# Leaving out the products that nothing reads, in the norms of a two-block transformer kernel

## The chip, the cores and the metric

One Trainium2 chip, one core of it. The metric is the device time of one execution of the whole program, in microseconds (us). PE is TensorE, DVE is VectorE, ACT is ScalarE, POOL is GpSimd, SP issues the loads.

## The reference

Two models run one after the other on 272 and then 256 positions of width 1024. The first has two layers: differential attention with a SwiGLU, then a two-way RWKV-7 time mix with a mixture of eight experts; each half of a layer ends in a layer norm. The second has two layers of sparse attention beside a gated linear recurrence, each behind an rms norm, and a last rms norm at the end. The norms that matter here:

```python
def layer_norm(x, g, b):
    mu = jnp.mean(xf, -1, keepdims=True)
    var = jnp.mean(jnp.square(xf - mu), -1, keepdims=True)
    return ((xf - mu) * lax.rsqrt(var + LN_EPS) * g + b).astype(x.dtype)
...
h = layer_norm(DEEPNORM_ALPHA * h + mix, ln_g[i, 0], ln_b[i, 0])
...
h = layer_norm(DEEPNORM_ALPHA * h + ff, ln_g[i, 1], ln_b[i, 1])
...
    ym = jnp.mean(y, -1, keepdims=True)
    yv = jnp.mean(jnp.square(y - ym), -1, keepdims=True)
    y = ((y - ym) * lax.rsqrt(yv + RW_LNX_EPS)).reshape(B, L, D) * lnx_g + lnx_b
...
def rmsnorm(x, g):
    y = xf * lax.rsqrt(jnp.mean(xf * xf, axis=-1, keepdims=True) + NORM_EPS)
```

## The kernel before

The state is kept transposed in SBUF: `H` is 128 partitions x 8 slices x 272 positions, feature on the partition. Every weight comes from HBM in 1 MB loads, ACT rounds a piece to its high part (`wh`, line 301), DVE subtracts to get the low part (`wl`, line 310), and PE makes three products per tile (`mm3`, lines 158 to 160). Four such pieces are kept at a time: ACT may round piece n only when PE has used piece n-4.

A sum over features is a product with a matrix of ones. In a layer norm (`norm_pe`) PE sums `H` (line 436), DVE centres it (L473), ACT squares it (L452), PE sums the squares (L443), DVE scales and adds the epsilon (L479), ACT takes the root (L456), DVE the reciprocal (L481), and DVE and ACT make the eight slices of the next input (L489, L462, L486, L464), on which the next stage's first products wait. The rms norm (`rms_pe`, L2272) is the same without the centring. The norm over heads in the time mix sums squares at L1180, makes the root and reciprocal (L1544, L1321, L1547), and then goes slice by slice: PE spreads the reciprocal (L945), DVE multiplies (L1554, L1557, L1560), PE makes the next gate product (L1187, L1188).

Each of these norms ends, on PE, in a call of `busy_pe`: five (over heads: three) fp32 products of the identity with 512 columns of constants into a PSUM bank. Their semaphore `busy` is waited for only by a later product that takes the same bank.

PSUM has eight banks. `bank()` hands them out in turn, from 0 to 7 and again, unless the caller names one, and returns who held the bank before; the caller waits until that holder's result has been read:

```python
    def bank(event, *key, b=None):
        if b is None:
            b = turn[0] % 8
            turn[0] += 1
        before, holder[b] = holder.get(b), (event, *key)
```

In the attention of the second model the banks are named: scores in 0 and 1, the turned scores in 2, their products with the values in 3, and beside them eight units of `ma` and then `rnn` in 4 to 7 (units 4 to 7 of `rnn` last). `ga`, the eight units ahead of the attention, and `out_a`, the eight behind it, take banks in turn. On DVE the last steps of the attention stand in this order:

```python
            low(dve, SB)
...
            if n in (13, 19):
                for i in range(4):
                    rnn_gate(i + 4 * (n // 19))
```

so `rnn_gate(4)` to `rnn_gate(7)` (L2821), which read the banks of `rnn` 4 to 7, come behind the last two `low` steps (L310). Nothing else orders PE against them before `out_a`: PE waits there for the attention's own result, its weights and its bank. All orders are written out by hand; there is no scheduler.

Of the kernel before, what the change touches and what calls it, by code (L numbers as in the profile page):

```python
# [162 lines left out]
def build(nc, A, out, known=None, stages=99):  # L163
# [15 lines left out]
    def tile(name, cols, dt=F32):  # L179
        o = top[0]  # L180
        top[0] += -(-cols // 8) * 32
        return at_offset(name, o, cols, dt)
# [7 lines left out]
    PAR, CB = tile("PAR", NPAR), tile("CB", 592)  # L190
# [7 lines left out]
    PS = nc.alloc_psum_tensor("PS", [128, 8, 512], F32)  # L198

    ident = CB[:, 0:128]  # L200
# [12 lines left out]
# [5 lines that stand above are left out]
        bank_of[(event, *key)] = b  # L218
        return b, before
# [197 lines left out]
    top[0] = ARENA  # L417
    LNQ, LNR, LNS = tile3("ln_sq", KC, T), tile("ln_r", T), tile("ln_s", T)

    def busy_pe(pe, n, *key, at=None):  # L420

        b, before = bank("busy", *key, b=at)
        if before:
            pe.wait_ge(pe.at(*before))
        for i in range(n):
            t = pe.e.matmul(PS[:, b, :], ident, CB[:, 0:512], start=True, stop=True)
        t.then_inc(*pe.sig("busy", *key))

    def norm_pe(pe, key, after, Tn=T):

        b, before = bank("ln_sum", key)
        if before:
            pe.wait_ge(pe.at(*before))
        for k in range(KC):
            pe.wait_ge(pe.at(after, k))
            t = pe.e.matmul(PS[:, b, 0:Tn], ones, H[:, k, 0:Tn], start=k == 0, stop=k == KC - 1)
        t.then_inc(*pe.sig("ln_mm", key, "sum"))
        b, before = bank("ln_var", key)
        if before:
            pe.wait_ge(pe.at(*before))  # L440
        for k in range(KC):
            pe.wait_ge(pe.at("ln_sq", key, k // 2))
            t = pe.e.matmul(PS[:, b, 0:Tn], ones, LNQ[:, k, 0:Tn], start=k == 0, stop=k == KC - 1)  # L443
        t.then_inc(*pe.sig("ln_mm", key, "var"))
        busy_pe(pe, 5, key)

    def norm_act(act, key, hi=None, st=None):

# [80 lines left out]
    def attention_pe(pe):  # L529
# [74 lines left out]
        for i in range(4, KC):  # L604
            project_unit(pe, SA, "attn_o", i, 128, at_xs, T)
        norm_pe(pe, 0, "attn_o")

    def attention_act(act):
# [159 lines left out]
    def ffn_pe(pe):  # L768
        for _ in project_units(pe, SA, "gate", [("gate", 0), ("gate", 1), ("up", 0), ("up", 1)], ff_x, T, ("x_lo", "ln", 0)):
            pass  # L770
        for f0 in range(2, FFN // 128, 2):
            for what in ("gate", "up"):
                for j in range(2):
                    project_unit(pe, SA, what, f0 + j, 128, ff_x, T)
        for _ in contract_pe(pe, SA, "down", FFN // 128, ff_h, T, ("ff_lo",)):
            pass
        norm_pe(pe, 1, "down")
# [160 lines left out]
    def rwkv_pe(pe):  # L938
# [42 lines left out]
        for u in range(KC + 2):  # L981
            if u == 2:
                b, before = bank("k_norm")
# [11 lines left out]
        for j, w in enumerate([128, 32]):  # L995
            b, before = bank("gate_h", j)
            pe.wait_ge(pe.at(*before))
            for k in range(KC):
                pe.wait_ge(pe.at("mixed", 5, k))
                t = e.matmul(PS[0:w, b, 0:T], gv[:, k, j * 128:j * 128 + w], MIXED[5][:, k, :], start=k == 0, stop=k == KC - 1)  # L1000
# [3 lines left out]
        for f in range(KC):  # L1004
            b, before = bank("k_spread", f)
# [5 lines left out]
        def take(event, *key, b=None):  # L1011
            b, before = bank(event, *key, b=b)
            pe.wait_ge(pe.at(*before))
            return b
# [151 lines left out]
        for c in range(4):  # L1166
            for f in (2 * c, 2 * c + 1):
                take("bonus_v", c, b=f)
                t = e.matmul(PS[:, f, 0:T], blk, bonus[:, f, 0:T], start=True, stop=True)
            t.then_inc(*pe.sig("bonus_mm", c))  # L1170
        pe.wait_ge(pe.at("y", len(groups) - 1))
        for c in range(4):
            for f in (2 * c, 2 * c + 1):
                take("y_mean", c, b=f)
                t = e.matmul(PS[:, f, 0:T], blk, rw_y[:, f, 0:T], start=True, stop=True)
            t.then_inc(*pe.sig("y_mean_mm", c))
        b = take("y_var", b=0)
        for f in range(KC):
            pe.wait_ge(pe.at("y_sq", f // 2))
            t = e.matmul(PS[0:16, b, 0:T], by_head[:, f, :], po_q[:, f, :], start=f == 0, stop=f == KC - 1)  # L1180
# [4 lines left out]
        def gate(f):  # L1185
            b = take("y_gate", f, b=2 + f % 2)
            e.matmul(PS[:, b, 0:T], slot[:, f * 128:(f + 1) * 128], gh[:, 0, :], start=True, stop=False)  # L1187
            e.matmul(PS[:, b, 0:T], slot[0:32, D + f * 128:D + (f + 1) * 128], gh[0:32, 1, :], start=False, stop=True).then_inc(  # L1188
                *pe.sig("y_norm_mm", f, "gate"))

        pe.wait_ge(pe.at("raw", "A", m))
        gate(0)
        gate(1)
        busy_pe(pe, 3, "y", at=1)
        pe.wait_ge(pe.at("y_var_r"))
        first_units = project_units(pe, SA, "rw_o", [("rw_o", i) for i in range(4)], po_y, T, ("x_lo", "rw_o"),
                                    (4, 5, 6, 7))
# [9 lines left out]
        for i in range(4, KC):  # L1207
            project_unit(pe, SA, "rw_o", i, 128, po_y, T)
        norm_pe(pe, 2, "rw_o")

    def rwkv_act(act):
# [1055 lines left out]
    def rms_pe(pe, l):  # L2267
        b, before = bank("rms_sum", l)
        pe.wait_ge(pe.at(*before))
        for k in range(KC):  # L2270
            pe.wait_ge(pe.at("rms_sq", l, k // 2))
            t = pe.e.matmul(PS[:, b, 0:SEQ], ones, rq[:, k, :], start=k == 0, stop=k == KC - 1)  # L2272
        t.then_inc(*pe.sig("rms_mm", l))
        if l < 2:
            busy_pe(pe, 5, "rms", l)

    def rms_act(act, l):
        for c in range(4):
# [32 lines left out]
    def second_pe(pe, l):  # L2311
        e = pe.e
        rms_pe(pe, l)
        for _ in project_units(pe, SB, "iq", [("iq", (l, u)) for u in range(4)], (hh, hl), SEQ, ("x_lo", f"hn{l}")):
            pass
# [141 lines left out]
        if l:  # L2457
            rms_pe(pe, 2)
# [482 lines left out]
    def stage_list(name):  # L2941
        none = lambda x: 0
        lists = {"pe": [attention_pe, ffn_pe, rwkv_pe, moe_pe, none, second_pe],
                 "act": [attention_act, ffn_act, rwkv_act, moe_act, none, second_act],
                 "dve": [attention_dve, ffn_dve, rwkv_dve, moe_dve, none, second_dve],
                 "pool": [none, none, rwkv_pool, moe_pool, none, second_pool]}[name]
        f = lists.pop()
        return (lists + [lambda x: f(x, 0), lambda x: f(x, 1)])[:stages]
# [136 lines left out]
```

## Time and profile before

| | us |
|---|---|
| median of 3 runs | 2882.27 (2877.8 to 2885.52) |
| the profiled execution, its own time | 2887.5 |
| its span, first to last instruction | 2885.7 |
| PE busy | 2687.2 (93%) |
| DVE busy | 2045.1 (71%) |
| ACT busy | 1541.5 (53%) |
| mean granted TensorE clock | 0.957 of full |

A busy share tells how much of the span an engine had work; which engine sets the time of a stretch is read from the waits. The granted clock is full (2.4 GHz) or half (1.2 GHz); a value between is a mean over a stretch.

### The profile page before, as it was taken

To read this page: it belongs to the slowest core of one execution; us is meant where nothing else is said; L and a number is where in the kernel's file an instruction comes from. 1 tells how busy PE (TensorE), PEld (TensorE's weight loads), DVE (VectorE), ACT (ScalarE), POOL (GpSimd) and SP (SyncE) were. 2 spreads that over 40 slices of the span, in tenths; PEclk is the share of its full clock that TensorE was granted. 3 is DMA by queue.
4 is the path that set the end of the run, shared out by engine and by line. 5 is a ranking of instruction groups with operands and counts; after the bars stand their busy time and mean duration, and the time that the engine had idled before them with its cause. 6 is when DMAs were issued, how large, how long until landed. Compare 5 with 4: busy or idle time off the path is not lost.

```text
span 2885.7 us, 49498 instructions
## 1 busy us (share of the span) xinstructions
PE 2687.2 (93%) x21078; PEld 2216.2 (77%) x21078; DVE 2045.1 (71%) x2943; ACT 1541.5 (53%) x2245; POOL 101.4 (4%) x124
## 2 busy tenths in 40 slices
PE   7779999999898999999999999998999989999988
PEld 7649997688876766666666666667969988978977
DVE  4565546664435889898898989895856865757864
ACT  3334442622123777777777777774446454446443
POOL 0000000010003100000000000000000101000001
PEclk9759999999988999999999999999999999999999
DMA  6203553300022799898999989893525634524532
GB/s 206 74 0 117 176 171 98 108 21 4 4 102 75 297 348 349 332 364 335 344 352 348 351 330 364 333 346 102 153 58 149 186 113 123 154 80 145 167 118 96
DMA packets 244413, 547.66 MB, mean 190 GB/s; under 512 B 24492, under 2 KB 187784, under 8 KB 200924
## 3 DMA queue, kind: packets, MB, share of 16 engines
q1 hardware_dynamic: 242204, 541.54, 53.3%
q8 instruction: 169, 2.77, 0.4%
q0 software_dynamic: 1984, 2.89, 0.4%
q14 instruction: 56, 0.46, 0.0%
HBM read 540.46 MB, written 1.05 MB: 188 GB/s over the span
## 4 chain that ended last, share of the span: by engine, by line
PE 75%; DVE 15%; ACT 6%; issue 2%; DMA 2%; DVEq 0%; SPq 0%; ACTq 0%
PE PS L158 20%; PE PS L160 20%; PE PS L159 20%; DVE wl L310 3%; ACT wh L301 3%; PE PS L1066 1%; PE PS L349 1%; PE PS L2379 1%; PE PS L1810 1%; PE PS L577 1%; DVE mix L1359 1%; DMA raw<-in_w_in 1%; DVE mix L1357 1%; PE PS L1836 1%; PE PS L1094 1%
## 5 line engine op out<-in xcount | busy, mean ns | idle before, releaser
L310 DVE TENSOR_TENSOR wl<-raw,wh 128x1024 fp32r<-128x1024 f32 (+2 forms) x630 | 746.3, 1189 | 411.5 <-ACT wh L301 392.7
L301 ACT ACTIVATE wh<-raw 128x1024 fp32r<-128x1024 f32 (+2 forms) x630 | 643.9, 1026 | 582.6 <-PE PS L160 534.5
L310 DVE TENSOR_TENSOR wl<-early,wh 128x1024 fp32r<-128x1024 f32 x384 | 466.8, 1225 | 55.6 <-ACT wh L301 35.2
L301 ACT ACTIVATE wh<-early 128x1024 fp32r<-128x1024 f32 x384 | 407.0, 1061 | 127.7 <-PE PS L160 118.7
L158 PE MATMUL PS<-b_hn_h,wh 128*128 128x256 f32 (+2 forms) x1312 | 378.5, 288 | 15.1 <-DVE wl L310 8.9
L160 PE MATMUL PS<-b_hn_h,wl 128*128 128x256 f32 (+2 forms) x1312 | 372.3, 284 | 0.0
L159 PE MATMUL PS<-b_hn_l,wh 128*128 128x256 f32 (+2 forms) x1312 | 371.7, 283 | 0.0
L158 PE MATMUL PS<-wh,xe_h 128*96 128x512 f32 x896 | 357.3, 399 | 1.2 <-DVE xe_l L1962 1.2
L160 PE MATMUL PS<-wh,xe_l 128*96 128x512 f32 x896 | 353.7, 395 | 0.0
L159 PE MATMUL PS<-wl,xe_h 128*96 128x512 f32 x896 | 353.4, 394 | 0.0
L158 PEld LDWEIGHTS PS<-b_hn_h,wh 128*128 128x128 f32 (+2 forms) x1312 | 233.4, 178 | 20.6 <-DVE wl L310 10.5
L159 PEld LDWEIGHTS PS<-b_hn_l,wh 128*128 128x128 f32 (+2 forms) x1312 | 233.2, 178 | 0.7
L160 PEld LDWEIGHTS PS<-b_hn_h,wl 128*128 128x128 f32 (+2 forms) x1312 | 233.1, 178 | 0.3
L160 PEld LDWEIGHTS PS<-wh,xe_l 128*96 128x96 f32 x896 | 144.8, 162 | 63.6
L158 PEld LDWEIGHTS PS<-wh,xe_h 128*96 128x96 f32 x896 | 145.1, 162 | 61.1 <-DVE xe_l L1962 1.5
L159 PEld LDWEIGHTS PS<-wl,xe_h 128*96 128x96 f32 x896 | 145.4, 162 | 59.3
L158 PE MATMUL PS<-wh,mh_h 128*96 128x512 f32 x448 | 177.8, 397 | 0.0
L160 PE MATMUL PS<-wh,mh_l 128*96 128x512 f32 x448 | 177.0, 395 | 0.0
L159 PE MATMUL PS<-wl,mh_h 128*96 128x512 f32 x448 | 175.8, 392 | 0.0
L158 PE MATMUL PS<-ff_x_h,wh 128*128 128x272 f32 x352 | 102.1, 290 | 0.5 <-DVE ff_x_l L486 0.3
L160 PE MATMUL PS<-ff_x_h,wl 128*128 128x272 f32 x352 | 101.8, 289 | 0.0
L349 PE MATMUL PS<-mix,raw 128*128 128x272 f32 x384 | 95.4, 410 | 6.8 <-DVE mix L1359 4.0
(473 smaller groups left out, 5127.8 us busy)
## 6 DMA issues: line engine op xcount, KB each, us to landing
early<-in_moe_in SPq DMA_DIRECT2D x128, 1024.0 KB, 4.8
raw<-in_moe_in SPq DMA_DIRECT2D x96, 1024.0 KB, 4.8
early<-in_moe_out SPq DMA_DIRECT2D x64, 1024.0 KB, 4.8
raw<-in_w_in SPq DMA_DIRECT2D x56, 1024.0 KB
raw<-in_moe_out SPq DMA_DIRECT2D x48, 1024.0 KB, 4.9
raw<-in_w_in SPq DMA_DIRECT2D x32, 704.0 KB
raw<-in_attn_w_in SPq DMA_DIRECT2D x12, 1024.0 KB, 5.5
raw<-in_rw_w_rkv SPq DMA_DIRECT2D x12, 1024.0 KB, 5.0
```

Of the source, the lines that this page charges most:

```text
L158: e.matmul(o, wh, xh, start=start, stop=False)
L159: e.matmul(o, wh, xl, start=False, stop=False)
L160: return e.matmul(o, wl, xh, start=False, stop=stop)
L301: act.e.activation(st.two(n)[0], st.raw(n), ACT.Copy).then_inc(*act.sig("hi", st.name, n, sem=f"hi_{st.name}"))
L310: dve.e.tensor_tensor(lo, st.raw(n), hi.bitcast(F32), SUB).then_inc(*dve.sig("lo", st.name, n, sem=f"lo_{st.name}"))
L349: t = pe.e.matmul(PS[:, b, 0:Tn], cols_view(256)(st.slot(m))[:, k, c:c + 128], X[:, k, :], start=k == 0, stop=k == KC - 1)
L577: t = e.matmul(PS[:, b, 0:T], at_v[0:kn, kt, h * 128:(h + 1) * 128], at_t[h % 2][0:kn, kt, :], start=kt == 0, stop=kt == 2)
L1066: x = e.matmul(PS[p:p + CB_, b, f * CB_:(f + 1) * CB_], lhsT[p:p + CB_, f, :], rhs[p:p + CB_, f, :], start=True, stop=True)
L1094: x = e.matmul(PS[p:p + CB_, b, f * CB_:(f + 1) * CB_], a_[d][p:p + 64, f, t], b_[d][p:p + 64, f, t], start=True, stop=True)
L1357: e.scalar_tensor_tensor(X, rw_e[:, k, 1:T + 1], par("mu", 48 + i * 8 + k), H[:, k, :], MUL, SUB).then_inc(*dve.own())
L1359: e.scalar_tensor_tensor(X, rw_e[:, k, 0:T], par("mu", i * 8 + k), X, MUL, SUB).then_inc(*dve.sig("mixed", i, k))
L1810: t = e.matmul(PS[0:CAP, b, :], P1[:, i, e_, :], Ht[x][:, i, c], start=i + x == 0, stop=i + x == 3)
```

## The change

The function `busy_pe` and its three calls are taken out. `norm_pe` runs four times, `rms_pe` calls it for layers 0 and 1 of the second model, and the time mix once: in all 6 x 5 + 3 = 33 products of 128x512 are left out. No instruction reads what they wrote.

```diff
-    def busy_pe(pe, n, *key, at=None):
-
-        b, before = bank("busy", *key, b=at)
-        if before:
-            pe.wait_ge(pe.at(*before))
-        for i in range(n):
-            t = pe.e.matmul(PS[:, b, :], ident, CB[:, 0:512], start=True, stop=True)
-        t.then_inc(*pe.sig("busy", *key))
-
     def norm_pe(pe, key, after, Tn=T):
...
         t.then_inc(*pe.sig("ln_mm", key, "var"))
-        busy_pe(pe, 5, key)
...
         gate(0)
         gate(1)
-        busy_pe(pe, 3, "y", at=1)
         pe.wait_ge(pe.at("y_var_r"))
...
         t.then_inc(*pe.sig("rms_mm", l))
-        if l < 2:
-            busy_pe(pe, 5, "rms", l)
```

On PE, at the end of the first layer norm (`ff_x` is the input of the SwiGLU, whose products come next), there stood before:

```order
L443 MATMUL PS<-ln_sq,CB 128x272 [waits ln_act]
L443 MATMUL PS<-ln_sq,CB 128x272
L426 MATMUL PS<-CB 128x512 x5
L158 MATMUL PS<-ff_x_h,wh_56 128x272 [waits lo_A,x_lo_dve]
L159 MATMUL PS<-ff_x_l,wh_56 128x272
```

and there stands now:

```order
L434 MATMUL PS<-ln_sq,CB 128x272 [waits ln_act]
L434 MATMUL PS<-ln_sq,CB 128x272
L158 MATMUL PS<-ff_x_h,wh_56 128x272 [waits lo_A,x_lo_dve]
L159 MATMUL PS<-ff_x_l,wh_56 128x272
```

The five products between the last sum and the first product of the next stage are gone; the other sites look alike, and no row of DVE, ACT, POOL or SP moves.

`busy_pe` took a bank in turn at each of the six norms, so each call left out also moves every later product that takes a bank in turn one bank back. The first row of each of the eight `out_a` units in layer 0 of the second model, on PE (a unit is 24 products; `b_attn_dve` is what DVE counts up in the attention, `lo_B` the low parts of the weights), was before:

```order
L158 MATMUL PS<-b_o_246,wh_60 128x256 [waits lo_B,b_attn_dve]
...
L158 MATMUL PS<-b_o_246,wh_62 128x256 [waits lo_B]
...
L158 MATMUL PS<-b_o_246,wh_56 128x256 [waits lo_B]
...
L158 MATMUL PS<-b_o_246,wh_58 128x256 [waits b_attn_dve,lo_B]
...
L158 MATMUL PS<-b_o_246,wh_60 128x256 [waits b_attn_dve,lo_B]
...
L158 MATMUL PS<-b_o_246,wh_62 128x256 [waits b_attn_dve,lo_B]
...
L158 MATMUL PS<-b_o_246,wh_56 128x256 [waits b_attn_dve,lo_B]
...
L158 MATMUL PS<-b_o_246,wh_58 128x256 [waits lo_B]
```

and is now:

```order
L158 MATMUL PS<-b_o_246,wh_60 128x256 [waits b_attn_dve,lo_B]
...
L158 MATMUL PS<-b_o_246,wh_62 128x256 [waits b_attn_dve,lo_B]
...
L158 MATMUL PS<-b_o_246,wh_56 128x256 [waits b_attn_dve,lo_B]
...
L158 MATMUL PS<-b_o_246,wh_58 128x256 [waits b_attn_dve,lo_B]
...
L158 MATMUL PS<-b_o_246,wh_60 128x256 [waits lo_B]
```

The run of four waits for DVE stood at units 3 to 6 and stands at units 0 to 3.

## Rows read from the trace of the kernel before

**Rows 1.** The page: busy share by engine, and the chain that ended last.

```profile
PE 2687.2 (93%) x21078; PEld 2216.2 (77%) x21078; DVE 2045.1 (71%) x2943; ACT 1541.5 (53%) x2245; POOL 101.4 (4%) x124
PE 75%; DVE 15%; ACT 6%; issue 2%; DMA 2%; DVEq 0%; SPq 0%; ACTq 0%
```

**Rows 2.** Source line 426, the products left out (duration in ns min/median/max).

```profile
L426 PE MATMUL PS<-CB x66: 592/592/697, 250.9 to 2437.4; 128*128 128x512 f32 x66
```

**Rows 3.** Timeline, end of the first layer norm: start, us, engine, line, [idle before <- releaser].

```profile
250.89 4.46 PE L426 MATMUL PS<-CB 128*128 128x512 f32 x10
255.66 0.36 PE L158 MATMUL PS<-ff_x_h,wh 128*128 128x272 f32 x1 [0.31 <-DVE ff_x_l L486]
```

**Rows 4.** Timeline of PE behind the norms at 464, 903, 1975 and 2434 us.

```profile
472.86 7.50 PE L349 MATMUL PS<-mix,raw 128*128 128x272 f32 x25 [3.96 <-DVE mix L1359]
903.01 4.45 PE L426 MATMUL PS<-CB 128*128 128x512 f32 x10
907.30 5.58 PE L1684 MATMUL PS<-raw,H 128*96 128x8 f32 x48
1983.62 5.41 PE L2272 MATMUL PS<-b_rms_q,CB 128*128 128x256 f32 x16 [4.21 <-ACT b_rms_q L2281]
2437.94 0.36 PE L158 MATMUL PS<-b_hn_h,wh 128*128 128x256 f32 x1
```

**Rows 5.** Busy time by stretch: PE, PEld, DVE, ACT, POOL, then PEclk, DMA share, GB/s.

```profile
472.56:475.97 3.41, 3.11 (x7) 2.44 (x8) 3.27 (x10) 0.00 (x0) 0.00 (x0) 0.50 0.34 110
1984.67:1988.08 3.41, 3.41 (x10) 2.70 (x9) 1.23 (x1) 1.40 (x2) 0.00 (x0) 0.50 1.02 351
1993.30:1998.00 4.70, 4.70 (x40) 4.70 (x40) 4.55 (x13) 2.51 (x6) 0.00 (x0) 1.00 0.00 0
2401.94:2407.90 5.96, 5.96 (x28) 5.96 (x29) 0.01 (x1) 0.42 (x1) 2.12 (x3) 0.50 0.56 176
605.00:620.00 15.00, 11.62 (x129) 9.86 (x130) 11.42 (x32) 2.52 (x6) 0.00 (x0) 1.00 0.00 1
844.70:868.50 23.80, 22.19 (x69) 13.32 (x68) 7.15 (x16) 1.76 (x5) 0.00 (x0) 0.50 0.02 9
```

**Rows 6.** Waits of PE from the first SwiGLU product to its end, 255 to 456 us.

```profile
PE PS L158 <- DVE ff_x_l L486: 0.3, 1, 0.3
PE PS L158 <- DVE wl L310: 0.2, 1, 0.2
```

**Rows 7.** Timeline of the norm over heads.

```profile
837.96 2.84 PE L426 MATMUL PS<-CB 128*128 128x512 f32 x6
842.05 0.67 PE L945 MATMUL PS<-r,CB 16*64 16x272 f32 x4 [1.25 <-DVE r L1547]
846.50 1.17 PE L945 MATMUL PS<-r,CB 16*64 16x272 f32 x4
```

**Rows 8.** Timeline, `out_a` of layer 0 begins, and DVE's steps beside it.

```profile
2375.95 2.58 DVE L310 TENSOR_TENSOR wl<-raw,wh 128x1024 fp32r<-128x1024 f32 x2 [1.58 <-ACT wh L301]
2376.01 0.28 PE L158 MATMUL PS<-b_o,wh 128*128 128x256 f32 x1
2378.44 1.41 DVE L2821 TENSOR_TENSOR b_m<-b_m,PS 128x256 f32<-128x256 f32 x4
```

**Rows 9.** The same, layer 1.

```profile
2821.08 0.28 PE L158 MATMUL PS<-b_o,wh 128*128 128x256 f32 x1
2823.52 1.40 DVE L2821 TENSOR_TENSOR b_m<-b_m,PS 128x256 f32<-128x256 f32 x4
```

**Rows 10.** Timeline of PE: stalls of 0.6 to 3.2 us, four places.

```profile
605.68 1.86 PE L1037 MATMUL PS<-CB,sc_n 128*128 128x128 f32 x14 [0.58 <-ACT rw L1216]
610.34 7.57 PE L349 MATMUL PS<-mix,raw 128*128 128x272 f32 x32 [2.80 <-DVE sc_lb L1458]
2289.88 0.46 PE L2414 MATMUL PS<-b_k,b_q 128*128 128x128 f32 x2 [1.51 <-ACT b_iq L2467]
2401.94 0.55 PE L158 MATMUL PS<-b_q_r,wh 128*128 128x256 f32 x1 [3.16 <-DVE wl L310]
```

## The prediction

> **What bounds the kernel now.** I read the page first, then the source line of the products that go, then the timeline around each of their seven sites, then busy time and granted clock by stretch, then the waits. The page is to show that PE sets the time nearly everywhere: it is busy for 93% and holds 75% of the chain that ended last [rows 1]. So what stops PE or slows its clock is paid in full, and what it does while it would wait anyway is free. The source line shows the products left out: 66 rows, two per fp32 product, so 33 products [rows 2]. The timeline of the first layer norm shows ten such rows in 4.46 us from 250.89 to 255.35, and the first product of the SwiGLU at 255.66, released by DVE after PE had stood idle for 0.31 us [rows 3]. The products therefore fill a pause that DVE and ACT make, and hold nothing up. At 464 and at 1975 us PE idles for another 3.96 and 4.21 us behind them [rows 4].
>
> **What goes, and what it was worth.** Ten rows take 4.46 us, so 66 take about 29 us of PE time, all of it in pauses; its removal gives back nothing directly. Only behind the norm at 903 us do they end as the next product starts (903.01 + 4.45 = 907.46, and the router starts at 907.30 [rows 4]); there the gain is at most some tenths of a us, and I take none.
>
> What the pauses now do to PE's clock is the first term. The stretches show three things. Behind the norms at 464 and at 1975 us, where PE idled for 4 us, the clock fell to half, 1.2 GHz, for 3.41 us each time (472.56 to 475.97 and 1984.67 to 1988.08 [rows 5]). Where the left-out products filled the pause up to the next product, it stayed at 2.4 GHz (1993.30 to 1998.00 reads 1.00 [rows 5]). And a product of 256 columns takes 5.96/28 = 0.213 us at half clock, 4.70/40 = 0.118 us at full [rows 5], so each us at half loses 0.45 us. After the change PE idles for about 4.5 us at 251 us (250.9 + 0.2 to 255.66 [rows 3]) and equally long in the two rms norms at 1989 and 2434 us. These are pauses like the two that brought a fall. At 464 us the first product ran at 472.86, so 3.1 us of work lay in the slow stretch; at 1975 us all 3.4 us. I take 3.2 us at half, 1.4 us lost, at each of three sites: 4.3 us. The bounds are 0 (the fall lies in the pause) and the longest such stretch behind a stall, 5.96 us, 2.7 us lost [rows 5], each: 0 to 8. Nothing makes it good later: from the first SwiGLU product to the stage's end PE waited only 0.3 + 0.2 us in 200 us [rows 6]. At 464 and 1975 us the price is paid already, so nothing is added there.
>
> The Trainium skill (TensorE: Matmul & The Clock Gate, Terms) puts the loss at half of the time spent at half rate, by which three falls would cost 3 x 3.2 x 0.5 = 4.8 us; the rows give 4.3 and are used. The same page (HAM oscillation) says that pauses between bursts bring the lower clock and advises against leaving them, which speaks against this change; the trace agrees, by the two falls of 3.41 us.
>
> In the norm over heads the three products took 2.84 us, and 1.25 us of idleness followed [rows 7]. The clock was at half from 844.70 to 868.50 anyway [rows 5]. Without them it can fall earlier, and the first spread, on which DVE's first slice waits, would take the 1.17 us of the later one instead of 0.67 [rows 7]: 0.5 us. Bounds: 0, and 3.4 us more at half, 1.5.
>
> **What moves.** The second term is the banks. In layer 0 of the second model the run of four waits of `out_a` for DVE stands at units 3 to 6 before: the units take banks 1, 2, 3, 4, 5, 6, 7, 0, and banks 4 to 7 hold `rnn` 4 to 7. Five turns fewer (four layer norms, one rms norm) put unit 0 on bank 4. It must then wait for `rnn_gate(4)`, which stands behind two `low` steps on DVE. Before, PE began `out_a` at 2376.01, while DVE ran these two steps until 2378.5 and the first gate behind them (four in 1.41 us, about 0.4 each) [rows 8]. Unit 0 can now start only at about 2378.9: 2.9 us more. The `low` steps do not get earlier, since ACT rounds these pieces only when PE has used the last of `rnn`. In layer 1 unit 0 stood on bank 3; six turns back is bank 5, the gate of `rnn` 5. PE began at 2821.08, the second gate ends at about 2823.52 + 0.8 = 2824.3 [rows 9]: 3.2 us. All of `out_a` and what follows queues behind it. The next long stall, 3.16 us at 2401.94, waits for a `wl` [rows 10] whose piece follows the last unit of `out_a`, so it moves along and gives nothing back. Sum 6.1 us; bounds 0 (that stall takes it up) and 8 (the wait reaches the last gate).
>
> Such a stall can cost clock as well. The one of 3.16 us was followed by 5.96 us at half [rows 5, 10]; the one of 2.80 us at 610.34 by none, the stretch reads 1.00 [rows 5, 10]. I take one chance in two for each of the two new ones, times 1.5 to 2.7 us: 2.0 us together. Bounds 0 and 5.4.
>
> Two smaller moves: PE's wait of 0.58 us at 605.68 [rows 10] is for the bank of the fifth `r` unit, two places back it is an earlier unit's: 0.6 us less. The wait of 1.51 us at 2289.88 for the last `ga` unit's bank [rows 10] goes from layer 0, but in layer 1 the first `ma` unit comes to stand on that bank: nothing on balance, bounds -1.5 and 1.5. The other waits that change places in the scan name results that are there early or lie in front of a wait for the same DVE step; I take 0, bounds -1 and 1.
>
> Sum: 4.3 + 0.5 + 6.1 + 2.0 - 0.6 = 12.3 us. The profiled execution took 2887.5 us; 5.2 above the median of 2882.27, within about the spread of the three runs. On its own time the change gives 2899.8, on the median 2894.6; I say 2894.
>
> **The rivals.** A measurement of this kernel tells about 0.3%, 8.6 us, from no change.
>
> *The bank waits are hidden, only the clock is paid.* If `out_a`'s late start were taken up at the stall of 3.16 us [rows 10], 4.3 + 0.5 - 0.6 = 4.2 us remain: 2886.5. For it speaks that this stall is as long as the new one; against it, that its releaser is downstream of PE's own last unit. Chance 0.22.
>
> *The bank waits are paid, the clock does not fall.* The sums ahead of the pause and the dense products behind it might hold it up: 6.1 - 0.6 = 5.5, so 2888. Against it stand both falls at 472 and 1984 us [rows 5]. Chance 0.08.
>
> *Faster: the products did hold up real work.* The place is the first product behind each norm; the price is what of 29 us was not in a pause. It decides if PE was ready later than its data: 0.31 us of idleness at 255.66 [rows 3] says that it was not. Were half of it exposed, 2882 - 14 = 2868. Chance 0.04.
>
> *The slow stretch in the norm over heads gets longer.* It took 23.8 us at half [rows 5]. Should it last 15 us more, 15 x 0.45 = 6.8 us come on top of 12.3: 2901. Chance 0.04.
>
> *Forecast: both terms*, chance 0.62, its own range 2889 to 2901.
>
> **How the numbers follow.** Faster is the third rival, 0.04. Within 0.3%, up to 2890.9, are the first two, 0.30, and the lower end of the forecast, where the clock terms come out small, 0.06: 0.36. Slower is the rest, 0.60. The range is 2885 to 2902: it takes in the first two rivals, for the most part, and leaves out the faster case, what lies below the first rival, and sums with both clock terms at their upper bounds, together 2 in 10.
>
> **What would show it.** In the changed kernel's timeline the first SwiGLU product stands behind about 4.5 us of idleness and still starts at the same distance from the reciprocal; a stretch of 5 us behind it, and behind the two rms norms, reads a PEclk clearly below 1.00. The first row of `out_a` shows an idle time of about 2.9 and 3.2 us, released by L2821's line. If the first lacks, the clock term is wrong; if the second lacks, or if the stall ahead of the next stage is shorter than 3.16 us by as much, the bank term is. A time under 2885 would say that both are.

## The result, and the profile after

| | before | changed |
|---|---|---|
| median | 2880.59 us (6 runs) | 2891.56 us (6 runs, 2888.57 to 2903.07) |
| ratio to before | | 1.0044, 95% interval 1.0023 to 1.0065 |
| the same, measured again with more runs | 2880.47 us (23 runs) | 2892.19 us (8 runs); 1.0037, 1.0022 to 1.0052 |
| profiled execution, its own time | 2887.5 us | 2903.07 us |

Leaving the products out costs 11 to 13 us. Forecast were 2894 us and 12.3 us more than before. The profiled execution of the changed kernel is the longest of its six, that of before lay 7 us above its median: one pair of profiles shows sites, not sums.

The page of the changed kernel, the two rows that answer to [rows 1]. PE has 18.7 us less work in a longer span, and its share of the chain is a point lower:

```profile
PE 2668.5 (92%) x21012; PEld 2213.3 (76%) x21012; DVE 2044.3 (70%) x2943; ACT 1540.5 (53%) x2245; POOL 97.0 (3%) x124
PE 74%; DVE 15%; ACT 6%; issue 2%; DMA 2%; DVEq 0%; SPq 0%; ACTq 0%
```

Timeline of PE in the changed kernel at the norms, at the scan and at the starts of `out_a`. Line numbers are 9 to 13 lower than before:

```profile
253.99 0.56 PE L158 MATMUL PS<-ff_x_h,wh 128*128 128x272 f32 x1 [4.60 <-DVE ff_x_l L476]
...
473.16 1.24 PE L349 MATMUL PS<-mix,raw 128*128 128x272 f32 x2 [8.26 <-DVE mix L1348]
...
608.18 2.99 PE L349 MATMUL PS<-mix,raw 128*128 128x272 f32 x12 [2.80 <-DVE sc_lb L1447]
...
900.28 3.93 PE L434 MATMUL PS<-ln_sq,CB 128*128 128x272 f32 x16 [1.51 <-ACT ln_sq L442]
908.28 7.99 PE L1673 MATMUL PS<-raw,H 128*96 128x8 f32 x48 [4.07 <-ACT H L454]
916.12 1.28 PE L1682 MATMUL PS<-CB,H 128*96 128x128 f32 x5
...
1986.79 6.44 PE L2261 MATMUL PS<-b_rms_q,CB 128*128 128x256 f32 x16 [8.50 <-ACT b_rms_q L2268]
1997.51 0.55 PE L158 MATMUL PS<-b_hn_h,wh 128*128 128x256 f32 x1 [4.27 <-DVE b_hn_l L2290]
...
2387.65 0.35 PE L158 MATMUL PS<-b_o,wh 128*128 128x256 f32 x1 [2.83 <-DVE b_m L2808]
2414.67 0.36 PE L158 MATMUL PS<-b_q_r,wh 128*128 128x256 f32 x1 [2.66 <-DVE wl L310]
2449.53 0.38 PE L158 MATMUL PS<-b_hn_h,wh 128*128 128x256 f32 x1 [4.28 <-DVE b_hn_l L2290]
...
2835.30 0.44 PE L158 MATMUL PS<-b_o,wh 128*128 128x256 f32 x1 [3.16 <-DVE b_m L2808]
```

The idle times in brackets are the pauses that the products had filled: 0.31 us is now 4.60 at the first SwiGLU product [rows 3], 3.96 is 8.26 at 473, 4.21 is 8.50 ahead of the rms norm [rows 4]. The router at 908.28 starts 8.00 us behind the sums of squares, as before (8.06: 907.30 [rows 4] less the 899.24 of this row of the kernel before), but its 48 thin products last 7.99 us where they lasted 5.58 [rows 4].

```profile
899.24 3.94 PE L443 MATMUL PS<-ln_sq,CB 128*128 128x272 f32 x16 [1.51 <-ACT ln_sq L452]
```

Both starts of `out_a` wait for L2808, which is `rnn_gate`, 2.83 and 3.16 us. The wait of 0.58 us ahead of the scan [rows 10] is gone.

Busy time by stretch in the changed kernel, columns as in [rows 5]; the seventh number behind the engines, PEclk, is the one to read:

```profile
251.60:258.30 6.70, 4.31 (x19) 4.34 (x20) 6.49 (x15) 5.51 (x14) 0.00 (x0) 0.50 0.00 0
470.00:476.80 6.80, 3.64 (x8) 2.83 (x9) 6.59 (x18) 1.71 (x5) 0.00 (x0) 0.50 0.20 59
907.00:920.50 13.50, 12.22 (x69) 11.87 (x70) 7.07 (x50) 7.80 (x19) 8.91 (x7) 0.50 0.24 81
1982.20:1992.20 10.00, 5.41 (x13) 4.34 (x14) 5.79 (x11) 6.44 (x13) 0.00 (x0) 0.50 0.47 150
1995.90:2002.50 6.60, 4.99 (x23) 5.02 (x24) 6.26 (x18) 3.32 (x8) 0.00 (x0) 0.50 0.00 0
2388.40:2391.60 3.20, 3.20 (x17) 3.20 (x17) 0.09 (x1) 0.73 (x1) 0.00 (x0) 0.50 0.96 316
2449.80:2453.00 3.20, 3.20 (x17) 3.20 (x17) 3.20 (x10) 1.93 (x5) 0.00 (x0) 0.50 0.00 0
2835.50:2838.70 3.20, 3.20 (x16) 3.20 (x16) 0.32 (x1) 0.96 (x1) 0.00 (x0) 0.50 0.93 308
```

Each pause over 4 us in the timeline above, and each of the two waits of `out_a`, has a stretch at 1.2 GHz behind it. The pause of 2.80 us at 608 has none (605 to 620 us reads 1.00). Two of the stretches, at 251 and 1996 us, are over 6 us long where 3.2 was forecast.

### The profile page after: what moved, and what is told of

It reads as the page before. It is cut to its first block, busy times and chain, and to the rows that moved or that the text cites. A ratio compares the mean times of both kernels' runs of the same rounds, so it can differ in the third digit from the quotient of the medians.

```text
span 2901.3 us, 49360 instructions
## 1 busy us (share of the span) xinstructions
PE 2668.5 (92%) x21012; PEld 2213.3 (76%) x21012; DVE 2044.3 (70%) x2943; ACT 1540.5 (53%) x2245; POOL 97.0 (3%) x124
## 4 chain that ended last, share of the span: by engine, by line
PE 74%; DVE 15%; ACT 6%; issue 2%; DMA 2%; DVEq 0%; SPq 0%; ACTq 0%
PE PS L158 20%; PE PS L160 19%; PE PS L159 19%; DVE wl L310 4%; ACT wh L301 3%; PE PS L1056 2%; PE PS L349 1%; DMA raw<-in_w_in 1%; PE PS L2366 1%; PE PS L567 1%; DVE mix L1348 1%; PE PS L1799 1%; DVE mix L1346 1%; PE PS L1825 1%; PE PS L1084 1%
```

## The experiments

The experiments ran in three groups, each with runs of the kernel before beside them (34, 23 and 35); a ratio is against those of its own group. In what follows a *shift* is the start of a PE row in a profile less the start of the same row in the profile of before, and a *step* is how much the shift grows across a site. Between two sites PE is mostly the bound, so the shift stays within 0.1 us for hundreds of us (in the changed kernel +0.29 us at 262 and at 455 us) and a step reads a site's price in one execution.

**Clock alone.** The products out, their bank turns kept:

```diff
         t.then_inc(*pe.sig("ln_mm", key, "var"))
-        busy_pe(pe, 5, key)
+        turn[0] += 1
```

(and the same in `rms_pe`). Expected:

> The 33 products are left out, but at each of the six norms one bank turn is still used up, so that every later product takes the bank it took before the change. Theory (two terms, clock and banks): only the clock term is left, 4.3 us for three pauses plus 0.5 us in the norm over heads, so about 4.8 us over the kernel before; no wait of out_a for L2821's gates; the rows behind the first layer norm and both rms norms at half clock. Rival one, the loss is all banks: within 1 us of the kernel before. Rival two, the loss is all clock: the whole 11 to 13 us that the change cost.

Measured: 1.0035 (1.0022 to 1.0048), 10.1 us over before. No start of `out_a` waits for L2821's gates. That is 6.3 to 13.8 us by the interval, so the clock term is about twice the 4.8 us that the theory gave; the run with `out_a` from bank 1, below, has 4.9 us for the same term less the scan, so its size is known to some 4 us only. The timeline and windows of this kernel at the first norm and behind the second rms norm:

```profile
254.55 0.57 PE L158 MATMUL PS<-ff_x_h,wh 128*128 128x272 f32 x1 [4.60 <-DVE ff_x_l L477]
```

```profile
253.00:259.60 6.60, 5.05 (x22) 5.08 (x23) 6.18 (x15) 6.25 (x16) 0.00 (x0) 0.50 0.00 0
2441.10:2447.50 6.40, 5.52 (x26) 5.55 (x27) 5.55 (x16) 3.17 (x8) 0.00 (x0) 0.50 0.00 0
```

**Rotation alone.** The products stay, outside the turn:

```diff
-        b, before = bank("busy", *key, b=at)
+        b, before = bank("busy", *key, b=(turn[0] - 2) % 8 if at is None else at)
```

> The 33 products stay, but take a bank whose result has been read long ago, outside the turn, so that every later product takes the bank that it has after the change. Theory: only the bank term, 2.9 + 3.2 us for the two starts of out_a, some 2 us of clock behind these two stalls, less 0.6: about 7.5 us over the kernel before (5.5 if the stalls bring no clock fall); first SwiGLU product without a half-clock stretch behind it. Rival one, the late start of out_a is taken up by the next stall: 0 to 1 us. Rival two, banks are all of it: 11 to 13 us. This and the run with the turns kept should add up to the change's cost.

Measured: 1.0036 (1.0022 to 1.005), 10.4 us. The first SwiGLU product had no slow stretch (step 0.0 us), both waits for the gates stood there. Waits of PE in this kernel, 2366 to 2372 and 2812 to 2824 us (us in total, times, longest), and the stretch behind the second:

```profile
PE PS L158 <- DVE b_m L2821: 2.8, 1, 2.8
PE PS L158 <- DVE b_m L2821: 3.2, 1, 3.2
```

```profile
2817.50:2824.00 6.50, 5.90 (x28) 5.93 (x29) 1.11 (x4) 2.10 (x2) 0.00 (x0) 0.50 0.51 161
```

Each of the two alone comes out near the whole change: 10.1 + 10.4 = 20.5 us, not 11 to 13. By these two runs the terms don't add up; the three intervals together leave some 6 to 7 us either way (an estimate, by adding their squares).

**`out_a` moved off the `rnn` banks** in the changed kernel:

```diff
+        turn[0] = 1
         for u in range(KC):
             projected(pe, l, "out_a", u, oT)
```

> The changed kernel, products left out, and the turn is set to bank 1 ahead of out_a in both layers, so that the first three units of out_a take banks 1, 2 and 3 and meet no bank of rnn 4 to 7. Theory: the waits of 2.9 and 3.2 us and the clock falls behind them go, 6 to 8 us less than the changed kernel, so 4 to 5 us over the kernel before. Rival, other places of the rotation cost as much as out_a: this run stays 8 us or more over the kernel before while the one with all turns kept does not.

Measured: 1.0017 (1.0001 to 1.0034), 4.9 us over before, in the theory's 4 to 5. Against the changed kernel's 1.0037 and 1.0044 two starts of `out_a` are worth 6 to 8 us. But it should equal the run with the turns kept, up to the 0.6 us ahead of the scan, and lies 5 us below it; the intervals overlap.

**Only `out_a` moved.** In the kernel before, all products kept, `turn[0] = 4 + l` at the same place:

> The kernel before, all products and turns kept, but out_a starts at bank 4 in layer 0 and at bank 5 in layer 1, as it does in the changed kernel. Theory: the price of the two starts alone, 4.6 + 4.8 us by the aligned profiles (of it 2.9 + 3.2 predicted as idleness, the rest half clock behind it), so 9 us over the kernel before, ratio 1.003. Rival (the rest of the rotation carried the loss of the run with the turns gone): 3 us or less.

Measured: 1.0033 (1.002 to 1.0047), 9.5 us (5.8 to 13.5). This is the cleanest price of the bank term. With the run before it, it makes up the whole change a second way: 4.9 + 9.5 = 14.4 us, which the intervals of the changed kernel hold (6.6 to 18.7 and 6.3 to 15.0 us). This pair does add up. Its timeline:

```profile
2373.79 0.36 PE L158 MATMUL PS<-b_o,wh 128*128 128x256 f32 x1 [2.83 <-DVE b_m L2822]
...
2822.57 0.55 PE L158 MATMUL PS<-b_o,wh 128*128 128x256 f32 x1 [3.16 <-DVE b_m L2822]
```

**Rotation without `out_a`.** The run with the turns gone, and `turn[0] = 1` ahead of `out_a`:

> The 33 products stay, the turns are gone as in the change, but out_a starts at bank 1 in both layers, so that it meets no bank of rnn. What is left is the rotation everywhere else. Theory (as predicted): 0.6 to 0.8 us less than the kernel before, by the bank wait in the scan, which a measurement can't tell from no change. Rival (the rotation hides a gain of some 5 us elsewhere): ratio 0.998 to 0.9985, and the wait at the start of out_a was then worth 14 us, not 9.

Measured: 0.9987 (0.9972 to 1.0003), 3.7 us under before with an interval that holds both answers: inconclusive. A later run (both fills, with this rotation, below) speaks against a gain.

**One site alone.** Only the third layer norm without its products, turn kept (`if key == 2: turn[0] += 1`, else `busy_pe`):

> The kernel before, with the five products left out in the third layer norm alone (903 us), its bank turn kept. The prediction said that there only some tenths of a us could be won, since the products end as the next one starts. Theory from the aligned profiles: PE now idles for 4.4 us, the clock falls before the router's products and the stretch from 903 to 912 us takes 2.3 to 2.6 us longer, all else alike. Rival: that loss came with the fall in another place, and here the stretch is 0.3 us shorter.

One execution, 2877.1 us. Timeline and windows of it behind that norm:

```profile
895.12 1.06 PE L1687 MATMUL PS<-raw,H 128*96 128x8 f32 x5 [4.06 <-ACT H L467]
```

```profile
882.00:894.00 12.00, 7.55 (x32) 5.62 (x30) 5.42 (x8) 2.98 (x5) 0.00 (x0) 1.00 0.00 0
894.30:907.60 13.30, 12.48 (x70) 12.11 (x71) 6.91 (x52) 7.93 (x20) 9.16 (x7) 0.50 0.26 86
```

The pause is 4.06 us, the clock falls in it, and the router runs at half: step 2.33 us, as in the changed kernel (2.34). But the pause isn't the only way to that state: of the eight other profiles that keep the products here, the runs with `out_a` alone moved and with the heads filled show steps of 2.33 and 1.60 us as well, one 0.88, and the mean of the eight is 0.7. So on average leaving the products out costs some 1.7 us here, by these profiles.

**Heads without their three products**, all else as before (`busy_pe(pe, 3, "y", at=1)` deleted):

> The kernel before, with only the three products in the norm over heads left out. Prediction's step: 0.5 us, by a slower first spread. Rival (they decide how long the slow stretch behind them lasts, 10 to 27 us in the profiles so far): 3 us or more over, the stretch at half clock in its profile above 24 us. Rival two: they do nothing, 0, within 1 us.

Measured: 0.9999 (0.9988 to 1.0009), which excludes the 3 us of the first rival but can't tell 0.5 us from nothing. In its timeline the first spread took the 1.17 us that the step named, behind 3.50 us of idleness, and the step over the whole stretch, 836 to 870 us, is 0.0:

```profile
842.91 1.17 PE L945 MATMUL PS<-r,CB 16*64 16x272 f32 x4 [3.50 <-DVE r L1546]
```

**More fill.** First nine products instead of five in the second and fourth layer norm:

```diff
-        busy_pe(pe, 5, key)
+        busy_pe(pe, 9 if key in (1, 3) else 5, key)
```

> The kernel before, with nine products of constants instead of five in the second and the fourth layer norm (464 and 1975 us), where PE idled for another 3.96 and 4.21 us. Four more take about 3.6 us. Theory (idle PE brings the half clock, filled pauses keep it): both falls of 3.41 us are gone, PEclk 1.00 behind them, 1.4 us less each, 2.8 us under the kernel before. Rival one, the fall comes from something else (weak load in the sums ahead): the stretches stay at 0.50 and the time is the same. Rival two, the added products end late and hold up the first product: up to 1 us over.

Measured: 1.0001 (0.9988 to 1.0014). The mechanism is right at both sites (460 to 480 us reads 1.00, and the step over the last layer norm and the rms norm is -1.67 us), and the time is the same. What was won is given back further on: from 545 to 606 us the clock is 0.97 in the kernel before and 0.92 here, and the shift grows by 3.3 us from 565 to 590. Over the whole stretch from 455 to 600 us the step is 3.1 to 3.2 us in the three profiles with this fill. In the six that keep five products there it is 0.0 once and -3.2 to -3.3 us five times, so the profile of before was itself a slow one here. Windows of the run with the longer fill:

```profile
460.00:480.00 20.00, 19.47 (x70) 12.89 (x69) 16.66 (x44) 5.38 (x11) 0.00 (x0) 1.00 0.06 20
545.00:606.00 61.00, 57.46 (x349) 40.09 (x348) 37.36 (x39) 21.28 (x37) 0.00 (x0) 0.92 0.21 70
568.50:581.90 13.40, 13.40 (x53) 7.06 (x52) 10.96 (x17) 1.39 (x3) 0.00 (x0) 0.63 0.23 79
```

Then the norm over heads, where the clock had been at half for 23.8 us [rows 5]:

```diff
-        busy_pe(pe, 3, "y", at=1)
+        busy_pe(pe, 5, "y", at=1)
...
                 spread(take("y_norm", f, b=f % 2), f).then_inc(*pe.sig("y_norm_mm", f))
+            if f < 2:
+                busy_pe(pe, 3, "y", f, at=7)
```

> The kernel before, with more products of constants in the norm over heads: five instead of three ahead of the first spread, and three behind the spread of slice 0 and of slice 1, where PE waits 1.61 us for DVE each time. Before, the clock was at half for 23.8 us there and a slice took 6.2 us; where a run had the clock at full it took 3.6 us. Theory (idle PE ahead of and between the slices brings the half clock): the half stretch is gone or cut to below 11 us, 7 to 10 us less than before, ratio about 0.997. Rival one (the thin products of 16 and 32 rows bring it, not idleness): the stretch stays at 24 us and the time is the same or up to 2 us longer. Rival two: the added products hold up the slices, 1 to 3 us longer.

Measured: 0.9986 (0.9975 to 0.9996), 4.0 us faster than before. Its windows and the spreads of three slices, now 3.59 us apart:

```profile
836.00:868.00 32.00, 31.75 (x156) 18.74 (x155) 15.07 (x33) 3.61 (x9) 0.00 (x0) 1.00 0.30 109
```

```profile
838.26 0.67 PE L945 MATMUL PS<-r,CB 16*64 16x272 f32 x4
838.86 2.84 PE L426 MATMUL PS<-CB 128*128 128x512 f32 x6
...
850.82 0.67 PE L945 MATMUL PS<-r,CB 16*64 16x272 f32 x4
...
854.41 0.67 PE L945 MATMUL PS<-r,CB 16*64 16x272 f32 x4
...
858.00 0.67 PE L945 MATMUL PS<-r,CB 16*64 16x272 f32 x4
```

The profile of before promised more, a step of -7.3 us from 836 to 870 us, but its slow stretch there was a long one. The kernels that are unchanged there have 10 to 24 us at half in their profiles and steps of 0.2, 0.0, -2.5, -5.9, -7.0 and -7.0 us (0.0 being before itself), -3.7 on average. The three with this fill have -7.3 each. The fill makes sure of what three of six came near without it, and the 3.6 us between the means fit the 4.0 measured.

Both fills together, and both with the rotation gone and `out_a` from bank 1:

> The kernel before with both longer fills: nine products in the second and fourth layer norm, five ahead of the first spread in the norm over heads and three behind each of its first two slices. Theory: the gains are independent, 3 to 4 us for the heads and 1.7 us for the last layer norm with the rms norm behind it: 5 to 6 us under the kernel before, ratio about 0.998. Rival: the fall only moves on to the next weak stretch, and the time is that of the run with the heads alone, 0.9986.

> Both longer fills, with the turns of the six norms gone and out_a from bank 1 in both layers: what won or did nothing so far, put together. Theory: the rotation is worth 0.8 us (the bank wait in the scan), so 6 to 7 us under the kernel before, ratio 0.9977. Rival (the rotation hides some 3 us, as the run with it alone had 0.9987): 9 us under, 0.997.

Measured: 0.9991 (0.9981 to 1.0001) and 1.0003 (0.9993 to 1.0013), 2.6 us under and 0.9 us over before. The second fill adds nothing to the first (and brings the same fall at 569 to 582 us), and the rotation adds nothing either. Four pairs of runs differ by the rest of the rotation: -5.2 us (products out), -3.7 (products kept), +0.9 (`out_a` moved) and +3.5 (both fills). They show neither a gain nor a loss beyond the noise. Of all versions only the one with the heads alone has an interval wholly under the kernel before, and its upper end is 0.9996.

**The changed kernel again:**

> The changed kernel once more, with twice the runs. The sites of its profile add up to more than its time: aligned with the kernel before, it loses 2.0 us at the first layer norm, 2.4 ahead of the router, 4.4 in the last layer norm and the rms norm behind it, 1.5 in the second rms norm, 4.6 and 4.8 at the two starts of out_a, and wins 0.75 in the scan: 19 us, against 12.7 measured. Theory (the first measurement was low by chance): 1.0055 to 1.0066, 16 to 19 us. Rival (about 5 us come back somewhere that depends on both the missing products and the rotation, since the run with out_a from bank 1 was also some 5 us lower than its sites): 1.0044 again, 12 to 13 us.

Measured: 1.0037 (1.0022 to 1.0052), 10.7 us. The first measurement wasn't low by chance; the steps of one profile, taken as they are, add up to more than the time. Part of that is chance in the steps themselves, as the next table shows.

## Why the prediction was right in its sum, and where it wasn't

Steps across the sites, in us, each from the shifts of one profile:

| site (us in before) | changed | again | turns kept | products kept, turns gone | only `out_a` moved | forecast |
|---|---|---|---|---|---|---|
| first layer norm, 228 to 262 | 2.0 | 2.3 | 2.3 | 0.0 | 0.0 | 1.4 |
| ahead of the router, 900 to 912 | 2.3 | 2.3 | 2.3 | 0.4 | 2.3 | 0 |
| last layer norm and rms norm, 1960 to 2003 | 4.4 | 1.1 | 2.9 | 0.0 | 2.2 | 1.4 |
| second rms norm, 2415 to 2445 | 1.5 | 1.5 | 2.6 | 0.0 | 0.0 | 1.4 |
| `out_a` layer 0, 2374 to 2380 | 4.6 | 4.6 | 0.0 | 4.6 | 3.1 | 2.9 + 1.0 |
| `out_a` layer 1, 2818 to 2830 | 4.8 | 4.8 | 0.1 | 6.0 | 4.8 | 3.2 + 1.0 |

A column shows chance alone where its kernel is unchanged at the site. The run with only `out_a` moved is unchanged at the first four sites, and still has 2.3 and 2.2 us at two of them. Two places are free of this: at the first layer norm, and from 1988 to 2003 us (behind the products of the first rms norm), the steps are 2.0 to 2.3 and 2.1 to 2.2 us in all four profiles without the products, and 0.0 in all nine with them.

**Nothing held up.** Right. The products filled pauses; no stage starts earlier without them, the first SwiGLU product still follows DVE's last part, 4.60 us after the last sum.

**Clock.** The mechanism is right, the term was mis-sized: 4.8 us forecast with the heads, 10.1 measured for the run with the turns kept (6.3 to 13.8) and 4.9 for the one with `out_a` from bank 1 (0.3 to 9.8). Two parts of it failed. The step "I take 3.2 us at half, 1.4 us lost" took the length of the two falls in one profile. Behind the unchanged pause of 3.96 us at 470 us, six other profiles have five products ahead of it: one shows 3.4 us at half again, five show 6.8, as here with only `out_a` moved:

```profile
470.80:477.40 6.60, 5.82 (x13) 4.46 (x14) 6.35 (x17) 0.00 (x0) 0.00 (x0) 0.50 0.22 61
```

Without the products the stretches at 251 and 1996 us are over 6 us in all four profiles, and 2.0 to 2.3 and 2.1 to 2.2 us are lost, half as much again as forecast; only behind the second rms norm is it 3.2 us and 1.3 to 1.5 lost in three of the four, and 6.4 us and 2.6 in the run with the turns kept.

The step "Only behind the norm at 903 us ... I take none" left out a fourth site: there the products had no pause behind them in the trace of before, so I read their removal as a possible gain. It opened a pause of 4.07 us like the others, and the router's thin products run at half. "At 464 and 1975 us the price is paid already" is not refuted. The pause at 1975 us doubled to 8.50 us and the sums behind it took 6.44 instead of 5.41 us, but they took as long with the products in place and a pause of 4.21 us, in the run with only `out_a` moved:

```profile
1977.23 6.46 PE L2272 MATMUL PS<-b_rms_q,CB 128*128 128x256 f32 x16 [4.21 <-ACT b_rms_q L2281]
```

From 455 to 600 us the step is -1.6 us in all four profiles without the products; the seven that keep five there, before included, average -2.3, so some 0.7 us is added. The steps so corrected, 2.2 + 2.1 + 1.5 at the three forecast sites, 1.7 at the router and 0.7 here, put the clock term at about 8 us, an estimate.

**Heads norm.** 0.5 us forecast, -0.3 measured (-3.5 to 2.6): too small to be seen either way.

**Banks.** Right, but for half a us. Idle 2.83 and 3.16 us against 2.9 and 3.2, released by the gate that was named. The clock falls behind both in all three profiles that have both with the full rotation, and behind the second alone in the run with only `out_a` moved, seven times in eight; and the step above the idle time is 1.8 and 1.6 us in the changed kernel, where one chance in two of 1.5 to 2.7 was taken: 9.4 us where 8.1 were forecast, and 9.5 measured with `out_a` alone moved. The stall ahead of the next stage went from 3.16 to 2.66 us, so a sixth of the first wait came back, where the forecast had nothing. The wait of 0.58 us ahead of the scan went, as said; the step there is -0.75 us.

**The sum.** 12.3 forecast, 11 to 13 measured, but not by the forecast's terms: the clock costs more than its forecast, so that the sum came out as near is partly luck. Clock 10.1, banks 9.5 and scan -0.8 make 18.8, which is 6 to 8 us more than the change cost. Each of the three times is known to some 4 us either way, together about 7 (an estimate), so this gap is about as large as its own error. The other pair, 4.9 for the clock with the scan and 9.5 for the banks, makes 14.4 and leaves 2 to 4 us. The granted clock says the same. Its mean over the executions is 0.9602 before and 0.9536 with the turns kept, 0.9582 with the rotation alone; as time at half, twice the missing share times the span, that is 38 and 12 us more than before, and the changed kernel (0.9523 against 0.9592 in its group) has 40, not 50. For `out_a` from bank 1 (0.9545 against 0.9602) and `out_a` alone moved (0.9587 against 0.9597) it is 33 and 6, which do add up to 40. Whether anything comes back is therefore left open. That the slow stretches of one site swallow those of another, as the longer fill showed in the other direction, would explain it; no run separates it from chance.

**Rivals.** That the bank waits are hidden fell by the run with only `out_a` moved: 9.5 us where this rival had none. That the clock doesn't fall fell at six sites. The faster case had nothing for it in any run. That the slow stretch in the norm over heads gets longer isn't borne out: it lasted 27.1 and 16.8 us in the two profiles of the changed kernel against 23.8 before, and leaving out its three products alone cost no time that shows.

## What to carry to other kernels

Work that nothing reads may still be doing two jobs: keeping TensorE's clock up through a pause, and holding a place in a rotation of buffers. Take it out in two kernels, one that keeps the place and one that keeps the work, before believing either cause; here either alone came out near the cost of both. Take the length of a slow stretch from several profiles: one profile showed 3.4 us where most others showed 6.8. And ask what a removed operation leaves behind: where it ended just as the next one began, its removal opens a pause, it doesn't close one.

## What the runs showed of the hardware

- **Executions of one kernel differ mainly by the clock.** Over 34 executions of the kernel before (2871.92 to 2890.47 us), time against time at half speed has a correlation of 0.84 and a slope of 0.37 us per us. The Trainium skill (TensorE: Matmul & The Clock Gate, Terms) puts the loss at half of the time at half rate; the slope here is less. Slow time that lies in pauses would lower it so; no run separates that out.
- **One slow stretch isn't fixed by the code near it.** In the norm over heads the clock was at half for 23.8 us before [rows 5] and for some 10 us in the run with one norm without, whose code is the same there; the changed kernel, which leaves three products out there, had 27.1 us in one profile and 16.8 in its second. Rows of the last two and of the run with one norm without, in this order:

```profile
842.10:869.20 27.10, 23.45 (x72) 13.62 (x73) 8.97 (x20) 2.15 (x5) 0.00 (x0) 0.50 0.13 53
```

```profile
837.40:854.20 16.80, 11.53 (x33) 6.09 (x34) 7.01 (x13) 1.42 (x4) 0.00 (x0) 0.50 0.30 126
```

```profile
840.00:849.50 9.50, 7.90 (x25) 4.56 (x23) 3.58 (x8) 0.86 (x2) 0.00 (x0) 0.50 0.00 0
```

- **Filling a pause can move the fall instead of ending it**: 3.4 to 6.8 us at half gone at 470 us, and a stretch of 0.63 from 568.50 to 581.90 us, in all three profiles that have the longer fill in the second layer norm.
